# Up stage of a PEER layer: 32x32 block turns on VectorE in place of TensorE transposes, and an unsplit routing product

## The chip, the cores and the metric
One core of a Trainium2 chip runs one layer on 512 tokens. The metric is the device time of one execution in microseconds (us). The kernel before was timed three times: 4906.25, 4911.32 and 4913.47 us, median 4911.32 us.

## The reference, cut to what matters
The layer has a token-mixing half (attention, Fourier branch, output projection, layer norm) and a channel-mixing half. The second half, PEER, is what changes:

```python
def _peer(h, wq, keys, u, v):
    q = (hf @ wq).reshape(T, PEER_HEADS, 2, PEER_HALF)
    s = jnp.einsum('thpd,hpkd->thpk', q, keys)
    s1, i1 = lax.top_k(s[:, :, 0], 16);  s2, i2 = lax.top_k(s[:, :, 1], 16)
    cand_s = (s1[..., :, None] + s2[..., None, :]).reshape(T, 8, 256)
    cand_i = (i1[..., :, None] * 128 + i2[..., None, :]).reshape(T, 8, 256)
    top_s, pos = lax.top_k(cand_s, 16)
    idx = jnp.take_along_axis(cand_i, pos, axis=-1)
    w = jax.nn.softmax(top_s, axis=-1)
    a = jnp.einsum('td,thkd->thk', hb, u[ib])          # u: 16384 experts x 2048
    coef = wb * jax.nn.gelu(a, approximate=False)
    return jnp.einsum('thk,thkd->td', coef, v[ib])     # v: 16384 x 2048
```

All of it is fp32.

## The kernel before, in words
The order of work on each engine is written out by hand, engine by engine, with semaphores between them; there is no scheduler.

For 384 of the 512 tokens (TD) PEER is computed densely: every expert's activation is formed (the up stage), multiplied with a routing matrix that is zero but for the chosen experts, and multiplied with v (the down stage). The first 128 tokens (TS) instead gather the rows they chose.

**Up stage.** 128 blocks (NK) of 128 experts. For each block:
- SyncE loads 1 MB of u into `pu[s]`, one of two buffers (`pre_load`, L530 to L533), and stores the block's activations to DRAM (`pre_store`, L535 to L537). In its order stands load i+2, then store i, then load i+3. A load waits until the block that had the buffer is turned (`u_turned`); a store waits for gelu i (`gelu_set`).
- TensorE turns the 16 pieces of 128x128 into PSUM (`pre_turn`, L2175), a quarter of the next block ahead of each quarter of this one, and does the 48 products of the block with the activations in three split parts (`mm3`, L114 to L116: high times high, high times low, low times high). A quarter is 4 turns and 12 products.
- ScalarE copies the turned block to SBUF (`pre_copy`, L1049), rounds it to the high part (`pre_hi`, L1056) and takes the gelu of the product (`pre_gelu`, L1061). In one block (`top_block`, L1070) these stand: copy and high part of half 0 of block i+1, copy of half 1, gelu of block i, high part of half 1.
- GpSimd forms the low part (`u_low`, L698).

Beside the blocks run three other pieces of work, one after the other:
- Blocks 0 to 25 (P0 = 26): VectorE picks the experts (`top_experts`), once for each 128 tokens, four times.
- Blocks 26 to 49: routing. For each group of 4 tokens VectorE makes one-hot matrices (`one_hots`: four instructions of 128x512, L1651 to L1657), TensorE does 8 products (L2235, L2236), ScalarE copies them out (L1096) and SyncE stores 1 MB for each block (L544). Four groups go with each block.
- Blocks 50 to 127 (LATE = 50): GpSimd gathers 128 times 1 MB of u rows (`gather_u`, L707) into a ring of 4 buffers, and VectorE takes the dot products (L1673).

Earlier parts that the change touches: SyncE's loads of the output projection (L498 to L504), the layer norm output `xn2` (L1518), and the loads of the PEER query weights (`w2raw`, L518). Each of these has its channels in natural order, channel 128c + p in chunk c at partition p.

Of the kernel before, what the change touches and what calls it, by code (L numbers as in the profile page):

```python
# [55 lines left out]
TK_FIRST, TK_REST = 8, 6  # L56
P0 = TK_FIRST + TK_REST * DB
# [61 lines left out]
def layer_kernel(nc, a, out):  # L119
# [10 lines left out]
    with ctx:  # L130
# [3 lines left out]

        gelu_d = nc.dram_tensor("gelu_scratch", [P, NK, TD], fp32, kind="Internal").ap()
# [108 lines left out]
        smalls = sb("tk_smalls", 87.5, [P, 3, PH])
        wait_pad = sb("wait_pad", 87.875, [P, 1])
# [8 lines left out]
        chwh, chwl = sb("chwh", 200, [P, TD], f32r), sb("chwl", 201.5, [P, TD], f32r)  # L254
        oneJe = [sb(f"oneJe{s}", 84 + 2 * s, [P, 4, P]) for s in range(2)]
        oneI = [sb(f"oneI{s}", 40 + 2 * s, [P, 4, P], f32r) for s in range(2)]
        oneJh = [sb(f"oneJh{s}", 44 + 2 * s, [P, 4, P], f32r) for s in range(2)]
        oneJl = [sb(f"oneJl{s}", 48 + 2 * s, [P, 4, P], f32r) for s in range(2)]
        RT = 64
        route = [sb(f"route{s}", (168, 52)[s], [P, NK, RT]) for s in range(2)]  # L260

        pu = [sb(f"pu{s}", 136 + 8 * s, [P, D]) for s in range(2)]
        pT = sb("pT", 96, [P, DC, P])
        pTuh, pTul = sb("pTuh", 152, [P, DC, P], f32r), sb("pTul", 160, [P, DC, P], f32r)
# [8 lines left out]
        col = [sb(f"col{s}", 82 + 3 * s, [P, 2, TD], f32r) for s in range(2)]  # L273
# [7 lines left out]
        diag2 = sb("diag2", 200, [P, 4, P])  # L281
# [56 lines left out]
        tk_chain, iota_in, tk_diff, tk_exp, tk_chosen, ch_turned, ch_set, chw_hi, chw_set = (  # L338
            sem(n) for n in ("tk_chain", "iota_in", "tk_diff", "tk_exp", "tk_chosen", "ch_turned", "ch_set", "chw_hi", "chw_set"))
# [34 lines left out]
        def _(sp):
# [134 lines left out]
            wq_v = a["peer_wq"][0].rearrange("(c p) n -> p c n", p=P)  # L509
# [16 lines left out]
            flat = lambda t, k: t[bass.ds(k, 1)].rearrange("a j d -> (a j) d")  # L526
# [44 lines left out]
            for k in range(2):  # L571
                pre_load(LATE + 2 + k, k)
                route_store(GROUPS, 1, 2 * k)
                route_store(GROUPS, 1, 2 * k + 1)
                pre_store(LATE + k, k)
# [75 lines left out]
        def _(pool):  # L651
# [69 lines left out]
            k = 0  # L721
            for i in range(LATE + 2, NK):
                for h in range(2):
                    u_low(i, h)
                    if k < SLOTS and (2 * i + h) % 6 != 5:
                        gather_u(k)
                        k += 1
            while k < SLOTS:
                gather_u(k)
                k += 1  # L730
# [7 lines left out]
        def _(act):  # L738
# [291 lines left out]
            q_split(NO, 1, 16 * 49)  # L1030
            q_split(NO + 1, 0, 16 * 51)
# [763 lines left out]
        def _(pe):  # L1795
# [373 lines left out]
            def pre_turn(i, s, q):  # L2169
# [6 lines left out]
                if q % 2 == 1:  # L2176
                    mm.then_inc(u_turned, 1)
# [166 lines left out]
```

## Time and profile before

| | |
|---|---|
| median of the timed runs | 4911.32 us |
| span of the profiled execution, first to last instruction | 4908.6 us |
| TensorE busy | 4529.0 us, 92% |
| VectorE busy | 2830.0 us, 58% |
| ScalarE busy | 1645.8 us, 34% |
| GpSimd busy | 1578.3 us, 32% |
| first gelu of the up stage, last gelu | 2263.1 us, 3697.0 us |

The profile gives the profiled execution no time of its own beside this span; the span lies inside the scatter of the three timed runs. Busy time is the union of an engine's instructions. Matmuls overlap in the pipeline, so a row's duration says less than the distance from one start to the next. SPq is SyncE's queue: a row there is the issue of a transfer, not its landing.

### The profile page before, as it was taken

How to read it: one execution, taken by the hardware profiler on the slowest of the kernel's cores; microseconds unless marked ns; L12 is line 12 of the kernel's file. 1: busy time of each engine (PE TensorE's matmuls, PEld its weight loads, DVE VectorE, ACT ScalarE, POOL GpSimd, SP SyncE). 2: the span in 40 equal slices, each digit the busy share in tenths (PEclk: the TensorE clock that was granted, in tenths of full speed). 3: DMA queues.
4: the chain of work that ended last, by engine and by line, in shares of the span. 5: the costliest groups of instructions: out<-in, count | busy, mean ns of one | idle time of the engine just before them, and what ended most of it. 6: DMA issues, size and time to landing. Idle time of an engine off the chain costs nothing.

```text
span 4908.6 us, 61497 instructions
## 1 busy us (share of the span) xinstructions
PE 4529.0 (92%) x23115; PEld 3858.2 (79%) x23115; DVE 2830.0 (58%) x3097; ACT 1645.8 (34%) x1746; POOL 1578.3 (32%) x643
## 2 busy tenths in 40 slices
PE   7899998999989999599999998999997999999997
PEld 2587777777767877488999998999995777777776
DVE  1234665545436653657789944444444677787777
ACT  0322232333331121224446543444442233332232
POOL 0002332000002310223544557887782233323320
PEclk9899999999989999699999999999998999999998
DMA  8325664000015652453336677777776999989885
GB/s 283 100 77 174 181 184 142 16 30 30 32 39 156 187 173 66 137 167 108 117 110 151 167 225 282 292 292 286 291 282 228 358 335 336 333 330 337 340 331 177
DMA packets 652126, 967.09 MB, mean 197 GB/s; under 512 B 122203, under 2 KB 520595, under 8 KB 599571
## 3 DMA queue, kind: packets, MB, share of 16 engines
q1 hardware_dynamic: 610979, 680.35, 42.0%
q0 software_dynamic: 40928, 285.23, 15.6%
q8 instruction: 45, 0.74, 0.1%
q10 hardware_dynamic: 144, 0.52, 0.0%
q14 instruction: 30, 0.25, 0.0%
HBM read 896.82 MB, written 69.21 MB: 197 GB/s over the span
## 4 chain that ended last, share of the span: by engine, by line
PE 55%; DMA 14%; DVE 11%; issue 10%; POOL 5%; ACT 4%; SPq 1%; DVEq 0%; ACTq 0%; POOLq 0%
PE pp L114 16%; PE pp L116 15%; PE pp L115 15%; DMA gel<-gelu_scratch 11%; POOL pTul L698 4%; DVE acc L1686 3%; PE pp L2175 3%; DVE vDl L1407 3%; DMA wm<-in_w_mod_dram 1%; PE pp L1806 1%; DVE mred L1287 1%; PE pp L1964 1%; PE pp L2236 1%; PE pp L2235 1%; ACT wh L776 1%
## 5 line engine op out<-in xcount | busy, mean ns | idle before, releaser
L698 POOL TENSOR_TENSOR pTul<-pT,pTuh 128x1024 fp32r<-128x1024 f32 x256 | 743.0, 2902 | 508.6 <-ACT pTuh L1056 494.7
L114 PE MATMUL pp<-h2h,pTuh 128*128 128x384 f32 x2048 | 733.0, 358 | 18.5 <-POOL pTul L698 17.5
L114 PE MATMUL pp<-vDh,coh 128*128 128x512 f32 x1536 | 617.7, 402 | 94.3 <-DVE col L1407 93.7
L116 PE MATMUL pp<-h2h,pTul 128*128 128x384 f32 x2048 | 691.7, 338 | 0.0
L115 PE MATMUL pp<-h2l,pTuh 128*128 128x384 f32 x2048 | 690.1, 337 | 0.0
L1673 DVE SCALAR_TENSOR_TENSOR ring<-ring,h2tok 128x2048 f32<-128x2048 f32 x128 | 347.8, 2720 | 490.0 <-DMA ring<-in_peer_u_dram,sidx 489.5
L115 PE MATMUL pp<-vDl,coh 128*128 128x512 f32 x1536 | 610.9, 398 | 0.0
L116 PE MATMUL pp<-vDh,col 128*128 128x512 f32 x1536 | 610.1, 397 | 0.0
L674 POOL TENSOR_TENSOR mbuf<-mbuf,silu 128x2048 f32<-128x2048 f32 x64 | 261.1, 4080 | 1003.4 <-DMA mbuf<-in_w_mod_dram 1002.7
L712 POOL DMA_INDIRECT ring<-in_peer_v_dram,sidx x128 | 319.1, 2493 | 771.0 <-DVE acc L1686 752.9
L1126 ACT ACTIVATE vDh<-vraw 128x2048 fp32r<-128x2048 f32 x128 | 245.3, 1917 | 668.4 <-PE pp L116 409.8
L114 PEld LDWEIGHTS pp<-vDh,coh 128*128 128x128 f32 x1536 | 296.9, 193 | 179.5 <-DVE vDl L1407 63.6
L114 PEld LDWEIGHTS pp<-h2h,pTuh 128*128 128x128 f32 x2048 | 387.9, 189 | 27.9 <-POOL pTul L698 27.5
L1202 DVE TENSOR_TENSOR wl<-wraw,wh 128x2048 fp32r<-128x2048 f32 (+1 forms) x97 | 263.1, 2712 | 246.2 <-ACT wh L776 245.9
L1049 ACT ACTIVATE pT<-pp 128x1024 f32<-128x1024 f32 x256 | 265.3, 1036 | 396.8 <-PE pp L2175 395.3
L115 PEld LDWEIGHTS pp<-h2l,pTuh 128*128 128x128 f32 x2048 | 388.6, 190 | 0.0
L116 PEld LDWEIGHTS pp<-h2h,pTul 128*128 128x128 f32 x2048 | 386.6, 189 | 0.0
L116 PEld LDWEIGHTS pp<-vDh,col 128*128 128x128 f32 x1536 | 296.0, 193 | 63.6
L115 PEld LDWEIGHTS pp<-vDl,coh 128*128 128x128 f32 x1536 | 296.5, 193 | 61.0
L1407 DVE TENSOR_TENSOR vDl<-vraw,vDh 128x2048 fp32r<-128x2048 f32 x128 | 292.7, 2287 | 73.0 <-ACT vDh L1126 73.0
L2175 PE MATMUL pp<-ident,pu 128*128 128x128 f32 x2048 | 312.3, 276 | 17.9 <-DMA pu<-in_peer_u_dram 17.1
L114 PE MATMUL pp<-hxh,wh 128*128 128x512 f32 x784 | 315.1, 402 | 13.6 <-DVE wl L1202 9.8
(343 smaller groups left out, 8849.3 us busy)
## 6 DMA issues: line engine op xcount, KB each, us to landing
pu<-in_peer_u_dram SPq DMA_DIRECT2D x128, 1024.0 KB, 6.8
vraw<-in_peer_v_dram SPq DMA_DIRECT2D x128, 1024.0 KB
mbuf<-in_w_mod_dram SPq DMA_DIRECT2D x64, 1024.0 KB, 5.7
wraw<-in_w_in_dram SPq DMA_DIRECT2D x48, 1024.0 KB, 8.3
wt<-route_scratch SPq DMA_DIRECT2D x128, 384.0 KB
gel<-gelu_scratch SPq DMA_DIRECT2D x128, 384.0 KB
wm<-in_w_mod_dram SPq DMA_DIRECT2D x16, 2048.0 KB, 8.4
gelu_scratch<-act_g SPq DMA_DIRECT2D x128, 192.0 KB
```

What stands on the lines that cost most here:

```text
L114: pe.matmul(out, lh, rh, start=first, stop=False)
L115: pe.matmul(out, lh, rl, start=False, stop=False)
L116: return pe.matmul(out, ll, rh, start=False, stop=last)
L674: pool.tensor_tensor(mbuf[s][:, :, :], mbuf[s][:, :, :], silu[:, :, 0:1].to_broadcast([P, DC, P]), ALU.mult).then_inc(mu_prod, 1)
L698: pool.tensor_tensor(pTul[:, c, :], pT[:, c, :], pTuh[:, c, :].bitcast(fp32), ALU.subtract).then_inc(u_lo, 1)
L712: pool.indirect_dma_start(ring[k % 4][:, :], None, v_rows, bass.IndirectOffsetOnAxis(ap=sidx[:, k:k + 1], axis=0)).then_inc(ring_in[k % 4] ...
L1049: act.activation(pT[:, 8 * h:8 * h + 8, :], pp[h][:, :].rearrange("p (c j) -> p c j", c=8), ACT.Copy).then_inc(pre_raw, 1)
L1126: act.activation(vDh[s][:, :, :], vraw[s][:, :, :], ACT.Copy).then_inc(w_hi, 1)
L1202: dve.tensor_tensor(wl[s][:, 0:n, :], wraw[s][:, 0:n, :], wh[s][:, 0:n, :].bitcast(fp32), ALU.subtract).then_inc(w_lo, 1)
L1407: return dve.tensor_tensor(dst, src, hi.bitcast(fp32), ALU.subtract)
L1673: dve.scalar_tensor_tensor(out=chunks(ring[k % 4]), in0=chunks(ring[k % 4]), scalar=1.0, in1=h2tok[:, :, 0:TS], op0=ALU.mult, op1=ALU.mult ...
L2175: mm = pe.transpose(pb[q][:, P * (c % 4):P * (c % 4) + P], pu[s][:, P * c:P * c + P], ident[:, :])
```

## The change
- A load of a block is four transfers of 32 partitions each. Partition 32k + s takes channels 512k to 512k + 511 of experts s, 32 + s, 64 + s and 96 + s: pieces of 2 KB, where before each partition took one expert's whole row of 8 KB.
- VectorE turns the block in 32x32 squares, SBUF to SBUF, in two instructions of 128x1024 for each block (`u_turn`). TensorE's `pre_turn` and ScalarE's `pre_copy` are gone. `pT`, `pTul` and `pTuh` now have two buffers each; `pTul` lies in the same memory as `pT`.
- In this layout partition 32k + r of chunk c is channel 512k + 32c + r. So that the other operand has the same order, `xn2` is written in permuted order, the query weights are loaded by quarters of 32 partitions, and shift and scale go through DRAM once to be read back in the new order (`mod2`).
- The four `top_experts` run beside 40 blocks (TK = 10 each), with 20 turns placed between their steps; routing runs beside blocks 40 to 63, and the gathers beside blocks 66 to 127, two for each block and three for each of the first four.
- The routing weight is no longer split: four VectorE instructions of 128x128 make the weighted one-hot, one of 128x512 the other, and TensorE does 4 fp32 products in place of 8 of a split pair.

```diff
-TK_FIRST, TK_REST = 8, 6
-P0 = TK_FIRST + TK_REST * DB
+TK = 10
+P0 = TK * (DB + 1)
...
+            sp.wait_ge(mu_set, 3)
+            for w, at in enumerate((M_SH2, M_SC2)):
+                sp.dma_start(mod_d[w].rearrange("(c p) -> p c", p=P), modT[:, at:at + DC, 0],
+                             allow_slow_non_contiguous=True).then_inc(mod_kept, 16)
             sp.dma_start(ln_g[:, :], a["ln1_g"][0:1, :].to_broadcast([P, D])).then_inc(ln_in, 16)
             sp.dma_start(ln_b[:, :], a["ln1_b"][0:1, :].to_broadcast([P, D])).then_inc(ln_in, 16)
+            sp.wait_ge(mod_kept, 32)
+            for k in range(4):
+                for w in range(2):
+                    sp.dma_start(mod2[32 * k:32 * k + 32, w, :],
+                                 mod_d[w, QD * k:QD * k + QD].rearrange("(c r) -> r c", r=32),
+                                 allow_slow_non_contiguous=True).then_inc(mod_in, 16)
...
-                    sp.dma_start(w2raw[s][:, :, :], wq_v[:, :, bass.ds(i * (2 * P) + (1 - s) * P, P)]).then_inc(w_in_[s], 16)
+                    for k in range(4):
+                        sp.dma_start(w2raw[s][32 * k:32 * k + 32, :, :],
+                                     wq_v[k][:, :, bass.ds(i * (2 * P) + (1 - s) * P, P)]).then_inc(w_in_[s], 16)
...
             def pre_load(i, s):
                 if not isinstance(i, int) or i >= 2:
                     sp.wait_ge(u_turned, 2 * i - 2)
-                sp.dma_start(pu[s][:, :], flat(u_v, i)).then_inc(u_in[s], 16)
+                for k in range(4):
+                    sp.dma_start(pu[s][32 * k:32 * k + 32, :, :],
+                                 u_quarter[k][bass.ds(i, 1)].rearrange("a s b d -> (a s) b d")).then_inc(u_in[s], 16)
...
-            def pre_copy(i, h):
...
+            def pre_hi(i, s, h):
                 act.wait_ge(u_turned, 2 * i + h + 1)
+                if not isinstance(i, int) or i >= 2:
+                    act.wait_ge((u_half, a_done)[h], i - 1)
+                act.activation(pTuh[s][:, 8 * h:8 * h + 8, :], pT[s][:, 8 * h:8 * h + 8, :], ACT.Copy).then_inc(u_hi, 1)
...
-            def top_block(i, s, exp=None):
-                pre_copy(i + 1, 0)
-                pre_hi(i + 1, 0)
+            def up_block(i, s, exp=None):
+                pre_hi(i + 1, 1 - s, 1)
                 if exp is not None:
                     act.wait_ge(tk_diff, exp)
                     act.activation(best[:, :, :], best[:, :, :], ACT.Exp).then_inc(tk_exp, 1)
-                pre_copy(i + 1, 1)
+                pre_hi(i + 2, s, 0)
                 pre_gelu(i, s)
-                pre_hi(i + 1, 1)
...
+            def u_turn(i, s, h):
+                c = slice(8 * h, 8 * h + 8)
+                dve.wait_ge(u_in[s], 32 * (i - s) + 64)
+                if not isinstance(i, int) or i >= 2:
+                    dve.wait_ge((u_half, a_done)[h], i - 1)
+                dve.transpose(pT[s][:, c, :].rearrange("p c (b j) -> p b c j", b=4),
+                              pu[s][:, :, 256 * h:256 * h + 256].rearrange("p b (c j) -> p b c j", j=32)).then_inc(u_turned, 1)
...
+            def route_block(i, s, g):
+                one_hots(g, 0)
+                one_hots(g + 1, 1)
+                u_turn(i + 1, 1 - s, 1)
+                one_hots(g + 2, 0)
+                one_hots(g + 3, 1)
+                u_turn(i + 2, s, 0)
...
+            for i in range(LATE, NK):
+                if i + 1 < NK:
+                    u_turn(i + 1, (i + 1) % 2, 1)
+                for k in range(rows_before(i), min(rows_before(i) + 1, rows_before(i + 1))):
+                    dot(k)
+                if i + 2 < NK:
+                    u_turn(i + 2, i % 2, 0)
+                for k in range(rows_before(i) + 1, rows_before(i + 1)):
+                    dot(k)
...
-                    pe.matmul(o, oneJh[s][:, t, :], oneI[s][:, t, :], start=True, stop=False)
-                    mm = pe.matmul(o, oneJl[s][:, t, :], oneI[s][:, t, :], start=False, stop=True)
+                    mm = pe.matmul(o, oneJ[s][:, t, :], oneI[s][:, t, :], start=True, stop=True)
```

ScalarE in the first blocks of the up stage, before. `pT<-pp` is the copy out of PSUM, `pTuh<-pT` the high part, `act_g<-pp` the gelu of the block before the one whose parts stand around it.

```order
L1049 ACTIVATE pT<-pp 128x1024 [waits u_lo,u_turned]
L1056 ACTIVATE pTuh<-pT 128x1024 [waits u_half,pre_raw]
L1049 ACTIVATE pT<-pp 128x1024 [waits u_lo,u_turned]
L1061 ACTIVATE act_g_218<-pp 128x384 [waits g_stored1,a_done]
L1056 ACTIVATE pTuh<-pT 128x1024 [waits a_done,pre_raw]
```

The same place now:

```order
L1070 ACTIVATE pTuh_213<-pT_209 128x1024 [waits a_done,u_turned]
L1070 ACTIVATE pTuh_214<-pT_210 128x1024 [waits u_half,u_turned]
L1075 ACTIVATE act_g_216<-pp 128x384 [waits g_stored1,a_done]
L1070 ACTIVATE pTuh_214<-pT_210 128x1024 [waits a_done,u_turned]
L1070 ACTIVATE pTuh_213<-pT_209 128x1024 [waits u_half,u_turned]
L1075 ACTIVATE act_g_215<-pp 128x384 [waits g_stored0,a_done]
```

Before, the gelu of block i stood behind work on block i+1 alone. Now the row ahead of it is the high part of the first half of block i+2.

SyncE in the loop of the first stretch of the up stage, before. `pu` is the loaded block, `gelu_scratch` the store of a block's activations.

```order
L533 ISA [waits u_turned]
L533 DMA pu_212<-in_peer_u_dram 128x2048
L536 REGISTER_ALU
L537 ISA [waits gelu_set]
L537 DMA gelu_scratch<-act_g_217 128x384
L532 ISA
L533 ISA [waits u_turned]
L533 DMA pu_213<-in_peer_u_dram 128x2048
```

The same place now:

```order
L554 DMA pu_207<-in_peer_u_dram 32x4x512
L558 REGISTER_ALU
L559 ISA [waits gelu_set]
L559 DMA gelu_scratch<-act_g_215 128x384
L552 ISA
L554 ISA [waits u_turned]
L554 DMA pu_208<-in_peer_u_dram 32x4x512
L554 ISA
L554 DMA pu_208<-in_peer_u_dram 32x4x512
L554 ISA
L554 DMA pu_208<-in_peer_u_dram 32x4x512
```

The order of loads and stores is as before; each load is now four issues, with a register instruction ahead of each.

## Rows read from the trace of the kernel before

**Rows 1.** The page: the chain that ended last, by engine
```profile
PE 55%; DMA 14%; DVE 11%; issue 10%; POOL 5%; ACT 4%; SPq 1%; DVEq 0%; ACTq 0%; POOLq 0%
```

**Rows 2.** Busy us of PE, PEld, DVE, ACT, POOL; clock, DMA share, GB/s
```profile
2264.00:2520.00 256.00, 253.41 (x1605) 249.07 (x1604) 206.79 (x744) 124.57 (x139) 128.12 (x49) 1.00 0.34 122
2560.00:2860.00 300.00, 292.42 (x2059) 289.82 (x2058) 295.60 (x342) 180.54 (x193) 150.35 (x44) 1.00 0.64 158
2960.00:3680.00 720.00, 712.21 (x4428) 695.38 (x4429) 313.83 (x230) 314.50 (x345) 569.48 (x252) 1.00 0.76 285
```

**Rows 3.** Instructions that touch the gelu tile, duration min/median/max, first and last start
```profile
L1061 ACT ACTIVATE act_g<-pp x128: 491/492/494, 2263.1 to 3697.0; 128x384 f32<-128x384 f32 x128
```

**Rows 4.** TensorE in time order, start and us: one quarter, then a routing group
```profile
2352.24 0.60 PE L2175 MATMUL pp<-ident,pu 128*128 128x128 f32 x4
...
2352.85 0.34 PE L115 MATMUL pp<-h2l,pTuh 128*128 128x384 f32 x1
...
2354.77 0.60 PE L2175 MATMUL pp<-ident,pu 128*128 128x128 f32 x4
...
2601.96 0.22 PE L2235 MATMUL pp<-oneI,oneJh 128*128 128x128 f32 x1
...
2602.80 0.62 PE L2175 MATMUL pp<-ident,pu 128*128 128x128 f32 x4
```

**Rows 5.** SyncE's queue in time order, two blocks of the first stretch
```profile
2389.35 0.35 SPq L537 DMA_DIRECT2D gelu_scratch<-act_g  x1
2390.03 0.34 SPq L533 DMA_DIRECT2D pu<-in_peer_u_dram  x1
2399.41 0.35 SPq L537 DMA_DIRECT2D gelu_scratch<-act_g  x1
2400.53 0.34 SPq L533 DMA_DIRECT2D pu<-in_peer_u_dram  x1
```

**Rows 6.** From issue to landing of `pu` loads: 2240:2520, then 2950:3300
```profile
DMA to landing us min/median/max: 4.6/4.8/6.9
DMA to landing us min/median/max: 4.9/7.4/14.1
```

**Rows 7.** Transfers by line, whole span: count, KB each, median us to landing
```profile
w2raw<-in_peer_wq_dram SPq DMA_DIRECT2D x16, 1024.0 KB, 8.6
praw_kv<-in_w_ukv_dram SPq DMA_DIRECT2D x8, 1024.0 KB, 6.5
```

**Rows 8.** ScalarE, then SyncE, in time order, late in the up stage
```profile
3418.12 0.49 ACT L1061 ACTIVATE act_g<-pp 128x384 f32<-128x384 f32 x1 [1.15 <-PE pp L116]
3418.51 1.05 ACT L1056 ACTIVATE pTuh<-pT 128x1024 fp32r<-128x1024 f32 x1
3418.77 0.35 SPq L537 DMA_DIRECT2D gelu_scratch<-act_g  x1
```

**Rows 9.** VectorE in time order: first and last steps of one `top_experts`
```profile
2240.89 1.23 DVE L1600 COPY tk_sc<-score 128x2048 f32<-128x2048 f32 x1 [0.99 <-DMA iota<-in_k_iota_dram]
2297.13 2.29 DVE L1624 TENSOR_REDUCE tk_chosen<-tk_pick 128x128 f32<-128x2048 f32 x1
```

**Rows 10.** VectorE in time order, routing: one-hot steps, and one small TENSOR_SCALAR
```profile
2602.48 0.68 DVE L1657 TENSOR_TENSOR oneJl<-oneJe,chwl 128x512 fp32r<-128x512 f32 x1
2603.13 2.85 DVE L1651 TENSOR_TENSOR oneJe<-iota,chT 128x512 f32<-128x512 f32 x1
...
2279.19 0.22 DVE L1610 TENSOR_SCALAR tk_bpos<-tk_besti 128x128 uint32<-128x128 uint32 x1
```

**Rows 11.** Tiles `pTul` and `ring`, 2960:3690, ns min/median/max
```profile
L698 POOL TENSOR_TENSOR pTul<-pT,pTuh x139: 2375/2398/4514, 2969.9 to 3684.7; 128x1024 fp32r<-128x1024 f32 x139
L1673 DVE SCALAR_TENSOR_TENSOR ring<-ring,h2tok x117: 2280/2293/5167, 2958.9 to 3687.9; 128x2048 f32<-128x2048 f32 x117
```

**Rows 12.** The chain of waits in time order: output projection, and the late stretch
```profile
1784.26 10.34 DMA wraw<-in_w_out_dram
...
2943.52 17.56 DMA pu<-in_peer_u_dram
```

More of the change, by code:

```diff
@@ L252, in layer_kernel @@
         dots, scoef = sb("dots", 206, [P, SLOTS]), sb("scoef", 206.5, [P, SLOTS])
[L254 to L258, printed above, removed]
-        RT = 64
[L260 to L264, printed above, removed]
+        oneJ = [sb(f"oneJ{s}", 40 + 2 * s, [P, 4, P]) for s in range(2)]
+        oneI = [sb(f"oneI{s}", 44 + 2 * s, [P, 4, P]) for s in range(2)]
+        RT = 64
+        route = [sb(f"route{s}", (168, 48)[s], [P, NK, RT]) for s in range(2)]
+        pu = [sb(f"pu{s}", 136 + 8 * s, [P, 4, QD]) for s in range(2)]
+        pT = [sb(f"pT{s}", 152 + 8 * s, [P, DC, P]) for s in range(2)]
+        pTul = [sb(f"pTul{s}", 152 + 8 * s, [P, DC, P], f32r) for s in range(2)]
+        pTuh = [sb(f"pTuh{s}", (96, 80)[s], [P, DC, P], f32r) for s in range(2)]
         act_g = [sb(f"act_g{s}", (5.5, 204)[s], [P, TD]) for s in range(2)]
@@ L525, in _ @@
             v_v = a["peer_v"][0].rearrange("(i j) d -> i j d", j=NK)
-            flat = lambda t, k: t[bass.ds(k, 1)].rearrange("a j d -> (a j) d")
+            u_quarter = [u_v[:, :, QD * k:QD * k + QD].rearrange("i (b s) d -> i s b d", s=32) for k in range(4)]
             for ss in g_stored:
@@ L570, in _ @@
                 route_steps(r)
[L571 to L575, printed above, removed]
+            pre_load(LATE + 2, 0)
+            for k in range(4):
+                route_store(GROUPS, 1, k)
+            pre_store(LATE, 0)
+            pre_load(LATE + 3, 1)
+            pre_store(LATE + 1, 1)
             with sp.Fori(LATE // 2 + 1, LATE // 2 + 3) as i:
@@ L694, in _, with u_low @@
                     unit(s, 16 * m + 16)
-            def u_low(i, h):
+            def u_low(i, s, h):
                 c = slice(8 * h, 8 * h + 8)
                 pool.wait_ge(u_hi, 2 * i + h + 1)
-                pool.tensor_tensor(pTul[:, c, :], pT[:, c, :], pTuh[:, c, :].bitcast(fp32),
+                pool.tensor_tensor(pTul[s][:, c, :], pT[s][:, c, :], pTuh[s][:, c, :].bitcast(fp32),
                                    ALU.subtract).then_inc(u_lo, 1)
@@ L713, in gather_v @@
                     ap=sidx[:, k:k + 1], axis=0)).then_inc(ring_in[k % 4], 16)
-            with pool.Fori(0, LATE + 2) as i:
-                u_low(i, 0)
-                u_low(i, 1)
+            with pool.Fori(0, LATE // 2 + 1) as i:
+                for s in range(2):
+                    for h in range(2):
+                        u_low(2 * i + s, s, h)
             pool.wait_ge(tk_chosen, 2)
@@ L720, in _ @@
                 pool.wait_ge(ss, 64 * (TD // RT // 2) + 16)
-            k = 0
             for i in range(LATE + 2, NK):
[L723 to L730, printed above, removed]
+                for k in range(rows_before(i), rows_before(i) + 1):
+                    gather_u(k)
+                u_low(i, i % 2, 0)
+                for k in range(rows_before(i) + 1, rows_before(i + 1)):
+                    gather_u(k)
+                u_low(i, i % 2, 1)
             for k in range(SLOTS):
@@ L1617, in top_experts @@
                 for w in range(2):
+                    turn(14 + 3 * w)
                     tk.link(dve.tensor_tensor(
@@ L1620, in top_experts @@
                         iota[:, 0:TOPK].unsqueeze(1).to_broadcast([P, PH * TOPK, TOPK]), ALU.is_equal))
+                    turn(15 + 3 * w)
                     pv = pick[:, :, :].rearrange("p (h k) m -> p h k m", h=PH)
@@ L2165, in _, with pre_quarter @@
             mod_sum(63, 1, 6, 30)
-            def pre_turn(i, s, q):
-                if q == 0:
-                    pe.wait_ge(u_in[s], 8 * (i - s) + 16)
-                if q % 2 == 0 and (not isinstance(i, int) or i >= 1):
-                    pe.wait_ge(pre_raw, 2 * i - 1 + q // 2)
-                for c in range(4 * q, 4 * q + 4):
-                    mm = pe.transpose(pb[q][:, P * (c % 4):P * (c % 4) + P], pu[s][:, P * c:P * c + P], ident[:, :])
-                if q % 2 == 1:
-                    mm.then_inc(u_turned, 1)
-            def pre_up(i, s, q):
+            def pre_quarter(i, s, q):
                 if q == 0 and (not isinstance(i, int) or i >= 2):
@@ L2214, in _ @@
             pe.wait_ge(mu_set, 4)
-            for i in range(TK_FIRST):
+            for i in range(TK):
                 pre_block(i, i % 2)
```

232 lines of the change are left out of this document (121 added, 111 removed).

## The prediction, made before the changed kernel was run
> **What bounds the kernel now.** First the chain that ended last, by engine: TensorE has 55% of it [rows 1]. Then the busy time by stretch. The up stage has three: experts being picked, routing, and gathers. TensorE is busy for 253.4 of 256 us in the first and 712.2 of 720 in the last; in the routing stretch VectorE is the full one, 295.6 of 300 [rows 2]. Third, the place of the stage: from its first gelu at 2263.1 to its last at 3697.0 are 1433.9 us for 127 steps [rows 3]. The two TensorE-bound stretches take about 10.1 us a block: one quarter runs from 2352.24 to 2354.77, 2.53 us, four to a block [rows 4]. Last, the DMA queue, which is never full (share 0.34, 0.64, 0.76 [rows 2]), but whose order of issue I read closely: store i, then load i+3, ten us apart [rows 5].
>
> **What TensorE and VectorE gain and pay.** Between 2352.85 and 2354.77 stand 11 products, 0.174 us each; 12 of them make 2.09 us, so without the four turns and the change of operand a quarter loses 0.44 us and a block falls from 10.1 to 8.4 us. Over 128 blocks that is 220 us of TensorE time. In routing a group now takes 0.84 us (2601.96 to 2602.80 [rows 4]) for 8 products of 128 columns. No row shows a plain fp32 product of 128 columns with 128 rows; I take four of them as dear as the eight (bounds 0.4 and 1.7 us), so a block there needs 4 x (2.09 + 0.09 + 0.84 + 0.07) = 12.4 us.
> VectorE gets two turns a block. The trace has none. A 128x2048 copy takes 1.23 us, a 128x2048 reduce 2.29 us [rows 9]; for half that size 0.6 and 1.15 us, and a full 2.3 us if a turn took two passes. I take 1.2 us, nearest to the one-pass row. One picking of experts lasts from 2240.89 to 2299.42, 58.5 us [rows 9]; with 20 turns 83 us in 10 blocks, 8.3 a block. In routing, 16 small steps of 0.22, four wide ones of 0.68 and two turns are 8.6 us; the wide ones and GpSimd hold each other up (0.68 becomes 2.85 [rows 10]), and two `pTul` steps of 2.40 [rows 11] make it at most 13.4. Late: two dot products of 2.29 and two turns, 7.0 us, and again up to 4.8 behind GpSimd. ScalarE loses its copies and is idle half the time. So by busy times alone the stage would shrink.
>
> **What the new order makes of the loads.** Here I expect the end to be set. ScalarE now takes gelu i behind the high part of block i+2, half 0. That waits for its turn, the turn for load i+2; store i waits for gelu i; and load i+3 stands behind store i in SyncE's order. So load i+2 must land before load i+3 is issued: one load under way at a time, one round of this circle for each block. Before, gelu i waited only for block i+1, whose load had gone out a whole block earlier: two blocks for each round, and TensorE was the slower. The terms of one round:
> - gelu to issue of the store: 3418.12 to 3418.77, 0.65 us [rows 8]; store to load 0.68 and 1.12 us, mean 0.90 [rows 5]. Together 1.55 us.
> - Issue to landing. A load of whole rows lands in 4.8 us in the first stretch [rows 6]. The new one is four issues of 32 partitions in pieces of 2 KB. The nearest row is `praw_kv`, 1 MB in 2 KB pieces, 6.5 us; 512-byte pieces take 8.6 us [rows 7]. I take 6.5 and 0.3 for the later issues, 6.8 us; ends 4.8 and 8.6.
> - the turn 1.2; the high part 1.05 less the 0.1 by which ScalarE overlaps its steps [rows 8], 0.95; two hand-overs of 0.1.
> Sum 1.55 + 6.8 + 1.2 + 0.95 + 0.2 = 10.7 us, above TensorE's 8.4 and VectorE's 8.3. TensorE follows in the shadow, some 2 us idle a block.
> The Trainium skill (SBUF — State Buffer, Door 1: The DMA port swizzle) says that 32 partitions reach 8 of the 16 DMA ports: 189 GB/s against 328 at 1 MiB, and that several transfers do not add up. By it a load costs 2.3 us more than the whole-row one, 7.1 us, and the forecast would be some 30 us later; no row here shows a transfer of 32 partitions.
>
> **The sum, from first gelu to last.** 40 blocks of 10.7: 428 us. 24 of routing: circle 10.7 + one copy-out of about 1.1, TensorE 12.4, VectorE up to 13.4: I take 12.7, 305 us. 63 late: landing there was 7.4 in place of 4.8 us in the first part and somewhat less later [rows 6], so 2.3 on top: 13.0 us each, 819 us. Once, where the loads of v stand ahead, a load takes 17.56 us [rows 12], 12 more than usual, and is now on the circle: 12 us. The exponentials' table loads, four times 1.5: 6 us. Total 1570 against 1434: +136 us.
> Outside: SyncE now waits between the norm's loads and the next `wraw` load, a load that is on the chain (10.34 us from 1784.26 [rows 12]). Two stores of 2048 single numbers, their landing and eight issues put it off by about 10 us, and as the norm's rows are through by then it lands some 4 sooner: +6 us (ends 0 and 15). The first `w2raw`, in four parts, +2 us (the others have a whole block of slack). `xn2` may lose a faster mode, within 1 us each, inside the 6. The down stage is left as it is.
> Profiled span 4908.6 + 136 + 8 = 5053 us. The median stands 2.7 us above the span, inside the scatter, so I say 5050 us. That is slower by 2.8%.
>
> **Rivals.**
> 1. The circle is there, but loads land as quickly as now, 4.8 + 0.3 = 5.1 us, because engines and not the destination set their pace. For it: the first and last stretch move whole rows at a DMA share of 0.34. Rounds of 9.0 and 11.3 us, routing 12.4: 360 + 298 + 712 + 18 = 1388, -46; 4871 us. Between it and the forecast each us of landing is worth 103 us, and equality lies at 5.5 us. Against: both rows with smaller pieces are dearer.
> 2. No circle: the load runs ahead after all and the other engines decide. First stretch VectorE 8.3 with small waits, 8.7, 348 us; routing 12.4, 298; late, dots and `pTul` in turn 9.4, with hand-overs 9.8, 617 us, and 18: 1281, -153. With +8 outside 4766 us. For it stands only that the waits might be met early; against, the order of three queues, in which I find no way round.
> 3. Turns are dearer, 2.3 us. The circle gains 1.1 on 103 blocks: +113, 5165 us. For it: nothing in the trace says that a turn runs at the rate of a reduce. The Trainium skill (VectorE: DVE Perf Modes, The three transpose paths) gives 311 ns for 128x128 in 32x32 squares of bf16; eight of these would be 2.5 us, which by itself would put the time near 5185 us, and no row here shows one.
> TensorE's clock was granted in full in all three stretches [rows 2]. Idle for 2 to 5 us a block it may be cut at times; it has that much slack, so I put no price on it.
>
> **Chances and range.** Forecast 52% (own range 4950 to 5130), rival 1 20%, rival 2 14%, rival 3 14%. A difference of 0.2%, 10 us, is what can be told from none. Faster: rival 2 and most of rival 1, 0.28. Within: 0.04. Slower: 0.68. The range 4860 to 5180 leaves out rival 2 and the far end of rival 3, 2 in 10.
>
> **What would show it.** Right: load issues 10 to 11 us apart in the first stretch and 13 late; each turn of a first half released by the DMA; landing of the last quarter about 7 us after the first issue; TensorE busy for about 80% in the first stretch and 65% in the last; the chain running through `pu`, the turn, `pTuh`, the gelu and SyncE. Wrong: a load issued while the one before is under way; TensorE full at 8.4 us a block (rival 2); landing near 5 us (rival 1); a turn of 2 us or more (rival 3).

## The result and the profile after

The changed kernel takes 5054.99 us (median of 4 runs, 5044.2 to 5068.84); the kernel before takes 4910.3 us beside it. The ratio is 1.0288, 95% interval 1.0274 to 1.0303. Forecast were 5050 us and a ratio of 1.028. The profiled execution has a span of 5067.2 us, 12 us over the median, where the one of before lay within 3 us of its own median. So the traces differ by 158.6 us and the medians by 145, and what is read from the traces below is up to 14 us too much in sum.

The page of the changed kernel: busy time, share and instructions; then the chain that ended last, by engine.

```profile
PE 4391.1 (87%) x21067; PEld 3686.3 (73%) x21067; DVE 3052.9 (60%) x3412; ACT 1381.0 (27%) x1489; POOL 1591.9 (31%) x643
...
DMA 22%; DVE 13%; issue 7%; SPq 5%; PE 4%; ACT 1%; POOL 0%; DVEq 0%; ACTq 0%; POOLq 0%
```

The shares of this chain sum to 52%: it reaches back to 2362 us only, and can't be set against the 55% of TensorE in [rows 1], which are of a whole span. The chain within the up stage can, first before (2263 to 3697), then now (2293 to 3861):

```profile
by line: PE pp L114 15.9%; PE pp L116 15.5%; PE pp L115 15.5%; issue 14.9%; POOL pTul L698 12.6%; PE pp L2175 9.1%; PE pp L2236 2.8%; PE pp L2235 2.6%; POOL ring L707 2.5%; DVE oneJl L1657 1.9%; DMA pu<-in_peer_u_dram 1.9%; ACT pTuh L1056 1
...
by line: DMA pu<-in_peer_u_dram 35.0%; issue 16.4%; DVE oneJ L1700 8.7%; DVE pT L1607 8.7%; SPq L554 8.5%; ACT act_g L1075 2.7%; SPq L559 2.7%; DVE oneI L1701 1.3%; PE pp L115 1.2%; PE pp L116 1.1%; PE pp L117 1.1%; DVEq L1700 1.0%; SPq L56
```

TensorE's lines fall from 61% of the stage to about 3%, and the loads of `pu`, VectorE's steps and SyncE's queue take their place. The gelu tile and the three stretches of the changed kernel, columns as in [rows 2, 3]:

```profile
L1075 ACT ACTIVATE act_g<-pp x128: 467/473/539, 2293.8 to 3860.6; 128x384 f32<-128x384 f32 x128
```
```profile
2300.00:2740.00 440.00, 350.78 (x1874) 339.04 (x1873) 305.55 (x866) 109.07 (x130) 202.53 (x76) 0.93 0.46 108
2780.00:3060.00 280.00, 276.89 (x1739) 255.27 (x1738) 278.88 (x475) 136.05 (x152) 114.98 (x44) 1.00 0.76 171
3200.00:3840.00 640.00, 495.94 (x2551) 467.86 (x2552) 415.92 (x320) 132.66 (x160) 499.92 (x214) 0.95 0.94 278
```

The up stage takes 1566.8 us for 1433.9. In the first stretch no engine is full: TensorE is busy for 80% (350.78 of 440), and its granted clock, which was 1.00 before, averages 0.93: for short stretches it is at the lower of its two levels, 1.2 GHz. In the last it is busy for 77%. In the routing stretch VectorE is full, 278.88 of 280, and TensorE nearly so, 276.89.

One round of the first stretch, first SyncE's queue, then ScalarE and VectorE (start and us; in brackets idle time and its end), answering to [rows 5, 8]:

```profile
2397.20 0.37 SPq L559 DMA_DIRECT2D gelu_scratch<-act_g  x1
2398.12 2.27 SPq L554 DMA_DIRECT2D pu<-in_peer_u_dram  x4
2408.45 0.37 SPq L559 DMA_DIRECT2D gelu_scratch<-act_g  x1
2409.12 1.82 SPq L554 DMA_DIRECT2D pu<-in_peer_u_dram  x4
2419.58 0.37 SPq L559 DMA_DIRECT2D gelu_scratch<-act_g  x1
```
```profile
2406.85 1.06 ACT L1070 ACTIVATE pTuh<-pT 128x1024 fp32r<-128x1024 f32 x1 [4.82 <-DVE pT L1607]
2407.82 0.47 ACT L1075 ACTIVATE act_g<-pp 128x384 f32<-128x384 f32 x1
...
2405.57 1.25 DVE L1607 STREAM_TRANSPOSE pT<-pu 128x1024 f32<-128x1024 f32 x1 [0.38 <-DMA pu<-in_peer_u_dram]
...
2416.70 1.25 DVE L1607 STREAM_TRANSPOSE pT<-pu 128x1024 f32<-128x1024 f32 x1 [4.61 <-DMA pu<-in_peer_u_dram]
```

Load at 2398.12, landed at 2405.57 (7.45 us), turn, high part at 2406.85, gelu at 2407.82, store at 2408.45, next load at 2409.12: 11.0 us, every link right behind the last. The chain of waits says the same in one view, in time order:

```profile
2410.62 6.06 DMA pu<-in_peer_u_dram
2416.70 1.26 DVE pT L1607
...
2418.95 0.48 ACT act_g L1075
2419.58 0.37 SPq L559
...
2420.50 0.32 SPq L554
...
2422.00 5.99 DMA pu<-in_peer_u_dram
```

The reader sees a circle with one load in it. The last of the four issues stands 1.5 us behind the first and lands 6.0 us later.

### The profile page after: what moved, and what is told of

Same layout as the page of the kernel before. It is cut to its first block, busy times and chain, and to the rows that moved or that the text cites. A ratio compares the mean times of both kernels' runs of the same rounds, so it can differ in the third digit from the quotient of the medians.

```text
span 5067.2 us, 58390 instructions
## 1 busy us (share of the span) xinstructions
PE 4391.1 (87%) x21067; PEld 3686.3 (73%) x21067; DVE 3052.9 (60%) x3412; ACT 1381.0 (27%) x1489; POOL 1591.9 (31%) x643
## 4 chain that ended last, share of the span: by engine, by line
DMA 22%; DVE 13%; issue 7%; SPq 5%; PE 4%; ACT 1%; POOL 0%; DVEq 0%; ACTq 0%; POOLq 0%
DMA gel<-gelu_scratch 11%; DMA pu<-in_peer_u_dram 11%; DVE acc L1749 3%; DVE oneJ L1700 3%; DVE pT L1607 3%; SPq L554 3%; DVE vDl L1418 3%; PE pp L115 1%; PE pp L116 1%; PE pp L117 1%; ACT act_g L1075 1%; SPq L559 1%; SPq L608 0%; SPq L615 0%; DVE oneI L1701 0%
## 5 line engine op out<-in xcount | busy, mean ns | idle before, releaser
L721 POOL TENSOR_TENSOR pTul<-pT,pTuh 128x1024 fp32r<-128x1024 f32 x256 | 695.5, 2718 | 603.0 <-ACT pTuh L1070 601.6
L116 PE MATMUL pp<-h2l,pTuh 128*128 128x384 f32 x2048 | 711.0, 347 | 0.0
L117 PE MATMUL pp<-h2h,pTul 128*128 128x384 f32 x2048 | 711.0, 347 | 0.0
L115 PEld LDWEIGHTS pp<-h2h,pTuh 128*128 128x128 f32 x2048 | 404.8, 198 | 312.8 <-POOL pTul L721 286.3
L1607 DVE STREAM_TRANSPOSE pT<-pu 128x1024 f32<-128x1024 f32 x256 | 317.2, 1240 | 449.2 <-DMA pu<-in_peer_u_dram 385.7
L1070 ACT ACTIVATE pTuh<-pT 128x1024 fp32r<-128x1024 f32 x256 | 271.5, 1060 | 1146.7 <-DVE pT L1607 1146.4
L735 POOL DMA_INDIRECT ring<-in_peer_v_dram,sidx x128 | 337.2, 2634 | 752.5 <-DVE acc L1749 732.9
L116 PEld LDWEIGHTS pp<-h2l,pTuh 128*128 128x128 f32 x2048 | 405.7, 198 | 0.0
L117 PEld LDWEIGHTS pp<-h2h,pTul 128*128 128x128 f32 x2048 | 403.8, 197 | 0.0
L1725 DVE SCALAR_TENSOR_TENSOR ring<-ring,h2tok 128x2048 f32<-128x2048 f32 x128 | 359.2, 2810 | 0.0
L115 PE MATMUL pp<-hxh,wh 128*128 128x512 f32 x784 | 316.3, 404 | 13.7 <-DVE wl L1213 9.8
```

What stands on the lines that cost most here:

```text
L115: pe.matmul(out, lh, rh, start=first, stop=False)
L116: pe.matmul(out, lh, rl, start=False, stop=False)
L117: return pe.matmul(out, ll, rh, start=False, stop=last)
L721: pool.tensor_tensor(pTul[s][:, c, :], pT[s][:, c, :], pTuh[s][:, c, :].bitcast(fp32), ALU.subtract).then_inc(u_lo, 1)
L735: pool.indirect_dma_start(ring[k % 4][:, :], None, v_rows, bass.IndirectOffsetOnAxis(ap=sidx[:, k:k + 1], axis=0)).then_inc(ring_in[k % 4] ...
L1070: act.activation(pTuh[s][:, 8 * h:8 * h + 8, :], pT[s][:, 8 * h:8 * h + 8, :], ACT.Copy).then_inc(u_hi, 1)
```

## The experiments

The table sets them side by side. The ratio is to the kernel before, run on the same chip. The three columns on the right are the mean distance from one gelu's start to the next, in us, from the trace: blocks 0 to 40, 40 to 64, 64 to 127 (in e10, which has the block numbers of the kernel before, routing is blocks 26 to 49). In brackets is the median of blocks 20 to 30, the steady pace. In e6, e7 and e8 the pieces of u lie in another arrangement than the turns are made for, so their up products are not the layer's; the kind and amount of work are the same.

| kernel | us | ratio (95%) | first | routing | late |
|---|---|---|---|---|---|
| changed | 5055.0 | 1.0288 (1.0274-1.0303) | 11.7 (11.4) | 12.9 | 12.5 |
| e1 gelu first | 4899.4 | 0.9977 (0.9966-0.9988) | 9.5 (8.3) | 12.7 | 11.5 |
| e2 load ahead | 4866.4 | 0.9904 (0.9887-0.9922) | 8.9 (8.5) | 12.7 | 11.4 |
| e3 loads of rows late | 5048.8 | 1.0283 (1.0265-1.0302) | 11.8 (11.3) | 12.9 | 12.4 |
| e5 rows behind `w_out` | 5032.1 | 1.0237 (1.0216-1.0258) | 11.7 (11.3) | 12.9 | 12.5 |
| e4 128 partitions, 4 outermost | 6037.5 | 1.2294 (1.2273-1.2315) | 16.9 (16.6) | 18.0 | 22.6 |
| e6 one issue, 8 KB rows | 4890.7 | 0.9955 (0.9937-0.9973) | 9.6 (8.7) | 12.8 | 11.2 |
| e7 32 partitions, 8 KB rows | 4995.1 | 1.0161 (1.0139-1.0183) | 11.1 (10.6) | 12.9 | 12.0 |
| e8 128 partitions, 2 KB | 4928.5 | 1.0033 (1.0022-1.0044) | 10.2 (9.6) | 12.8 | 11.5 |
| e9 two queues | 4970.0 | 1.0133 (1.0110-1.0157) | 10.2 (9.6) | 12.8 | 12.1 |
| e10 before, unsplit routing | 4903.4 | 0.9989 (0.9978-1.0001) | - | 13.8 | - |
| e11 e1 + e2 + e5 | 4833.5 | 0.9852 (0.9836-0.9868) | 8.7 (8.3) | 12.7 | 11.2 |
| e12 e11, low parts first | 4836.0 | 0.9845 (0.9831-0.9859) | 8.7 (8.3) | 12.7 | 11.3 |

The code below is shortened.

**Is there a circle? e1 and e2.** Each opens it at another place, and changes no transfer and no arithmetic.

```
e1, up_block, and the same in route_part:
-                pre_hi(i + 2, s, 0)
                 pre_gelu(i, s)
+                pre_hi(i + 2, s, 0)
```


> The changed kernel with one swap on ScalarE: gelu i ahead of the high part of block i+2, half 0. Theory (circle through pu, turn, high part, gelu, store, next load): the circle is opened, two loads can be under way. First stretch from 11.7 to about 8.8 us a block (TensorE 8.4, VectorE 8.3), routing unchanged at 12.9 (VectorE bounds it), late stretch from 12.5 to about 10.5: 4830 us (4780 to 4880). Rival A (loads of 32 partitions share one path, two under way land half as fast each): first stretch about 9, late unchanged at 12: about 4940. Rival B (VectorE's fixed order bounds the blocks, not the loads): no change, 5055 within 15.


```
e2, SyncE, and likewise in its other loops:
+            pre_load(2, 0)
             with sp.Fori(0, P0 // 2) as i:
                 for s in range(2):
-                    pre_load(2 * i + 2 + s, s)
+                    pre_load(2 * i + 3 + s, 1 - s)
                     pre_store(2 * i + s, s)
```


> The changed kernel with SyncE's order shifted by one: load i+3 is issued before store i, not behind it; ScalarE's order stays. It opens the same circle at another place. Theory: the gain of the ScalarE swap within 60 us, so 4780 to 4890. If the ScalarE order alone were the trouble (gelu held back by late high parts, and not the load behind the store), this would stay above 4980. Rival B (VectorE's order): no change, 5055 within 15.

Measured: 4899 and 4866 us, 156 and 189 less than the changed kernel. That is the circle, and both rivals fall: the first stretch goes from 11.4 to 8.3 and 8.5 us a block, which is TensorE's own pace. In e2 the chain of waits of 2320 to 2600 runs through TensorE's products, where in the changed kernel (2320 to 2740) it ran through the loads (its chain starts at 2362, so some 10% of that window stands in no term):

```profile
by line: PE pp L115 23.8%; PE pp L116 23.6%; PE pp L117 23.6%; issue 5.9%; DVE tk_pick L1679 4.6%; DVE tk_pick L1673 4.2%; DVE tk_chosen L1681 3.2%; DVE tk_besti L1594 3.0%; DVE tk_best L1589 2.9%; DVE pT L1611 2.5%; DVE tk_chosen L1685 0.6
```
```profile
by line: DMA pu<-in_peer_u_dram 31.1%; issue 23.7%; SPq L554 9.0%; DVE pT L1607 8.5%; ACT act_g L1075 3.1%; SPq L559 2.8%; PE pp L115 1.7%; PE pp L116 1.6%; PE pp L117 1.6%; ACT L1075 1.2%; DVE tk_chosen L1677 1.1%; DVE tk_cand L1596 0.9%; 
```

e1 stays 20 us over the range I gave. Its steady pace is right, but blocks 20, 30 and 40, where a picking of experts ends, take 20 to 23 us in it and 13 to 17 in e2; why was not followed up.

The late stretch stops at 10.8 us in both, and there another pair of engines is full. GpSimd and VectorE of e2, in time order:

```profile
3398.60 2.39 POOL L725 TENSOR_TENSOR pTul<-pT,pTuh 128x1024 fp32r<-128x1024 f32 x1
3401.15 2.83 POOL L734 DMA_INDIRECT ring<-in_peer_u_dram,sidx  x1 [0.16 <-issue]
3404.00 2.39 POOL L725 TENSOR_TENSOR pTul<-pT,pTuh 128x1024 fp32r<-128x1024 f32 x1
...
3398.84 4.30 DVE L1729 SCALAR_TENSOR_TENSOR ring<-ring,h2tok 128x2048 f32<-128x2048 f32 x1
3403.08 1.23 DVE L1611 STREAM_TRANSPOSE pT<-pu 128x1024 f32<-128x1024 f32 x1
3404.24 4.30 DVE L1729 SCALAR_TENSOR_TENSOR ring<-ring,h2tok 128x2048 f32<-128x2048 f32 x1
```

A dot product of 2.29 us [rows 11] takes 4.30 beside GpSimd's step of 2.39, and the gather's issue 2.83 in place of the 0.96 that it takes where VectorE waits. Each half block is then 5.4 us on both engines. Windows of e11, 3200 to 3600: VectorE busy for 392.5 of 400 us, GpSimd for 383.2. A rival is the DMA engines, whose share is about 1 there. Here are the columns of [rows 2] for e2, and then for e6, which moves as much a second in whole rows:

```profile
3200.00:3600.00 400.00, 329.61 (x1769) 306.25 (x1767) 382.61 (x221) 90.98 (x109) 382.11 (x148) 1.00 1.03 306
...
3250.00:3600.00 350.00, 289.41 (x1559) 268.61 (x1557) 350.00 (x196) 81.36 (x98) 338.45 (x130) 1.00 0.81 308
```

In e6 the DMA share is 0.81, and the steady pace is 10.8 us all the same, with VectorE busy for all of the 350 us. So it is not the DMA engines.

**What does the landing cost? e4, e6, e7, e8, e9.** The circle stays, and the load's form changes.

```
e4:  for b in range(4):
+        dma(pu[s][:, b, :], u[i] as (k s) d)      # 4 x 32 rows: outermost 4
e6:  dma(pu[s] as p (b d), u[i])                   # one issue, 128 rows of 8 KB
e7:  for k in range(4):
+        dma(pu[s][32k:32k+32] as p (b d), u[i, 32k:32k+32])
e8:  for k in range(4):
+        dma(pu[s][:, k, :], u[i, :, 512k:512k+512])   # outermost 128
e9:  SyncE issues k = 0, 1 as before; ScalarE, behind gelu i, k = 2, 3
```


> The changed kernel with the same bytes of u in the same four issues of 2 KB pieces, but each issue fills all 128 partitions with one piece (cut by row group, not by channel quarter). Theory for the landing (what an issue of 32 partitions lacks is spread: its packets go to half of the destination's ways): landing of the last quarter falls from 7.5 to about 5.5 us, the circle by 2 us in the first and late stretch, 103 blocks: 4850 us (4820 to 4900). Rival 1 (the size of the pieces sets it): landing and time unchanged, 5055 within 20. Rival 2 (the number of issues sets it): the same as rival 1 here; rows in one issue would tell them apart.

> The changed kernel with each block of u loaded as before the change: one issue, 128 partitions, rows of 8 KB (the turns then work on another arrangement of u, so that the values of the up products differ; nothing of the work is left out). Theory (a faster landing is worth its time on the circle until TensorE or VectorE bounds): landing from 7.5 to about 5.2 us; first stretch 9.0 a block, late 10.8: 4870 us (4840 to 4910). Rival (the loads' landing does not set the pace): 5055 within 15.

> As the run before it, but in four issues of 32 partitions with rows of 8 KB (values as there). Theory (32 partitions of destination set the pace of the packets): no gain over the changed kernel, landing 7 to 7.5 us, 5050 within 20. Rival (pieces of 2 KB set it): the time of the run with one issue of whole rows, 4870, at most 40 more for three further issues.

> Four issues of 2 KB pieces, each over all 128 partitions, with 128 as the outermost count of both sides; where the earlier run of this kind had 4 outermost and only 4 completion packets for each issue, here 16 are expected (values differ as in the two runs before). Theory: landing 5.2 to 5.6 us, 4880 (4850 to 4920). Rival (size of the pieces): landing 7.5, 5055 within 20. If the earlier 11 us burst came from cutting by row group and not from the outermost 4, it returns here: 6040.

> The changed kernel, its circle left in place, but quarters 2 and 3 of each load are issued by ScalarE's DMA queue right behind gelu i (quarters 0 and 1 by SyncE behind the store, as they are), so that two issues of different partitions can be under way at once. Theory (each issue of 32 partitions is held by its own part of the destination, different parts add up): packets near 84 ns in place of 147, last landing about 5.5 us after SyncE's issue and ScalarE's half 1.5 us sooner: first stretch from 11.25 to 9.3 a block, late from 12.0 to 11: 4920 us (4890 to 4970). Rival (transfers of several queues do not add up, the sum of bytes takes the same 5.8 us): the earlier half alone gains about 1 us a block, 4960 to 5000. No gain at all, 5055, if the last issue's landing is set by SyncE's half.

e4 missed by a thousand us and taught most. It carries the bytes of the changed kernel to the same places, but each issue has an outermost count of 4, and the trace shows 4 small completion packets for it where the others have 16: four of the sixteen engines carry it. The queue's line of three kernels in 2300 to 2500 (packets, MB, share of 16 engines' time), the changed kernel, e4 and e8:

```profile
q1 hardware_dynamic: 12383, 21.42, 46.3%
```
```profile
q1 hardware_dynamic: 8020, 14.85, 19.8%
```
```profile
q1 hardware_dynamic: 14285, 24.70, 37.4%
```

Per MB the changed kernel spends 2.16% of the engines' time in these 200 us, e8 1.51% and e4 1.33%. So e4's packets are quick, but one engine has four times as many in a row: a load takes 11.4 us from its first packet to its last, where one of the changed kernel takes 5.8 and one of e8 4.4. The Trainium skill has the rule (DMA: Bandwidth & Descriptors, Why a DMA increments its semaphore by 16 and not by 1): the number of engines is the largest up to 16 that divides the slowest dimension of both sides. It agrees with the 4 and the 16 seen here. e8 has the same four issues of 2 KB pieces over all partitions with 128 outermost, and its steady pace is 1.8 us better than the changed kernel's. That is the price of 32 partitions; the kernel's time, 4928, is 8 us over the range I had given. The pieces of 2 KB cost 0.8 (changed kernel against e7). If the costs simply add, three more issues cost 0.1, what is left of the 0.9 between e8 and e6; no run tests that sum, since the 1.9 between e7 and e6 follows from the other three differences. e6's 8.7 also stands close to TensorE's 8.4, which may hide a part of its gain. The landing line of e6, 2350 to 2550, then of the changed kernel, one quarter each, 2300 to 2740:

```profile
DMA to landing us min/median/max: 4.6/4.8/5.8
```
```profile
DMA to landing us min/median/max: 3.8/5.1/6.3
```

The line of the changed kernel counts each quarter from its own issue; 1.5 us and the queue of the three before it come on top. Whole loads, from the first issue to the first turn, take 7.6 us in the changed kernel (median of 2300 to 2740), 6.8 in e7, 5.7 in e8 and 5.0 in e6 (2300 to 2600). e7's theory said "no gain" and e7 gained 60 us: pieces do count, as the prediction had it, but partitions count more. e6, at 4891, is the first rival of the prediction made real (4871): with the landing left alone the change would have gained 0.45%.

The Trainium skill (SBUF — State Buffer, Door 1: The DMA port swizzle) gives 189 GB/s for a 1 MiB transfer to 32 partitions and 328 to 128. The runs agree in direction and show less of it: 2.16% against 1.51% is a factor of 1.4, where the page's figures make 1.7.

e9 fell between: 4970 us, at the edge of the theory's window and in the rival's. The ScalarE half is issued 2.2 us ahead of SyncE's. In the round at 2434 its packets run from 2435.77 to 2438.93 and SyncE's from 2438.39 to 2441.61, so the two hardly overlap, and the run doesn't tell whether two queues add up. That stays open.

**The detour of the norm's rows: e3 and e5.**

```
e3:
-            sp.wait_ge(mod_kept, 32)
-            (the eight loads of mod2)
             with sp.Fori(1, DC // 2) as i:          # loads of w_out
             ...
+            sp.wait_ge(mod_kept, 32)
+            (the eight loads of mod2)
e5: as e3, and the wait for mu_set and the two stores into mod_d go there too
```


> The changed kernel, with the wait for the two stores of the norm's rows and their eight loads moved behind the loads of w_out. Theory: the detour holds up the third w_out load, which came 32 us later in the profile, 25 to 30 of them not there before; the time falls by 25 us (18 to 32), 5030. Rival (the third w_out load is late for other causes, as the xres load of 4 MB ahead of it): 0 to 6 us, as the prediction priced it.

> The changed kernel with both the two stores of the norm's rows (4096 packets of 4 bytes) and their eight loads behind the loads of w_out. With the loads alone moved the time fell by only 6 us, and the w_out loads were still late: the next issue took 23.3 us behind the stores. Theory now: it is the stores that fill the queues for 16 us; with them gone from ahead of w_out the time falls by 25 us (18 to 32), 5030. Rival: the rows are then late for the norm's affine step, which takes back what w_out gains: 5045 to 5060.

e3 gained 6 us, which its interval can't tell from nothing, where I had expected 25: my reason was wrong. Not SyncE's wait holds up `w_out`, but what is in the queues. SyncE of the changed kernel, of e3, of e5:

```profile
1788.31 1.36 SPq L508 DMA_DIRECT2D mod_scratch<-modT  x2
1789.72 1.16 SPq L510 DMA_DIRECT2D ln_g<-in_ln_g_dram  x1
1790.92 0.43 SPq L511 DMA_DIRECT2D ln_b<-in_ln_b_dram  x1
1808.09 7.76 SPq L515 DMA_DIRECT2D mod<-mod_scratch  x8
1816.19 0.41 SPq L520 DMA_DIRECT2D wraw<-in_w_out_dram  x1
```
```profile
1787.23 0.39 SPq L514 DMA_DIRECT2D wraw<-in_w_out_dram  x1
1787.89 23.31 SPq L516 DMA_DIRECT2D wraw<-in_w_out_dram  x1
```
```profile
1785.70 0.39 SPq L510 DMA_DIRECT2D wraw<-in_w_out_dram  x1
1786.88 6.38 SPq L512 DMA_DIRECT2D wraw<-in_w_out_dram  x1
```

The transfers by line on the changed kernel's page (KB each, us to landing) name the culprit:

```profile
mod_scratch<-modT SPq DMA_DIRECT2D x2, 8.0 KB, 16.4
```

The two stores are 2048 packets of four bytes each and take 16.4 us; two megabytes of `ln_g` and `ln_b` stand behind them, and of e3's two loads of `w_out` after these the second hangs for 23.31 us. With the stores moved too, in e5, it is 6.38 (6.23 before the change), the time falls by 23 us, and the rows are ready at 1945, long before the norm asks at 2003.

**The routing part alone, e10.**

```
the kernel before, with
-  oneJe, oneJh, oneJl by four wide steps; two f32r products per token
+  for t in range(4): dve.tensor_scalar(oneJe[:, t], iota, chT[:, 1, at], chT[:, 2, at], is_equal, mult)
+  pe.matmul(o, oneJe[:, t], oneI[:, t])      # plain fp32
```


> The kernel before with one part of the change alone: the routing products unsplit (four fp32 products a group for eight, four small VectorE steps and one wide one for four wide ones). Theory (four fp32 products cost TensorE as much as the eight, VectorE has slack to gain): TensorE bounds the 24 blocks at 4 x (2.53 + 0.84) = 13.5 us, from 13.9 before: -10 us, 4900 (4890 to 4912). Rival A: the fp32 products are dearer, 1.1 us a group: +1 us a block, 4935. Rival B: they cost half, 0.42: 11.8 a block, 4860.

4903.4 us, as the theory said: TensorE is busy for 300.00 us of 300 there, and four fp32 products cost it what the eight did. In the changed kernel it is VectorE that bounds this stretch. The chain of waits of 2780 to 3060 runs mostly through its steps:

```profile
by line: DVE oneJ L1700 47.8%; issue 20.8%; DVE pT L1607 10.1%; DVE oneI L1701 6.9%; DVEq L1700 5.2%; DMA route_scratch<-route 3.0%; DMA pu<-in_peer_u_dram 2.4%; SPq L554 1.0%; DVEq L1701 1.0%; ACT route L1107 0.8%; SPq L559 0.3%; ACT act_g
```

TensorE is not far behind: from one group of routing products to the next it takes 2.97 us at the least and 3.22 at the median, four to a block, which makes 11.9 and 12.9 us a block. VectorE, then GpSimd:

```profile
2859.14 3.17 DVE L1700 TENSOR_SCALAR oneJ<-iota,chT 128x128 f32<-128x128 f32 x4
2862.23 0.68 DVE L1701 TENSOR_TENSOR oneI<-iota,chT 128x512 f32<-128x512 f32 x1
2862.83 1.23 DVE L1607 STREAM_TRANSPOSE pT<-pu 128x1024 f32<-128x1024 f32 x1
2863.99 1.07 DVE L1700 TENSOR_SCALAR oneJ<-iota,chT 128x128 f32<-128x128 f32 x4
...
2858.87 2.59 POOL L721 TENSOR_TENSOR pTul<-pT,pTuh 128x1024 fp32r<-128x1024 f32 x1 [3.86 <-ACT pTuh L1070]
```

Four small steps take 1.07 us, and 3.17 where GpSimd's step runs: 2 x (3.17 + 1.07 + 2 x 0.68 + 1.23) is 13.7, and less the overlaps of neighbours the 12.9 us of a block. No opening of the circle moved it: the steady blocks of e1, e2 and e11 take 12.9 too.

**A version that beats both: e11 and e12.**

> The changed kernel with the gelu swap, the load ahead of the store, and the norm's rows behind w_out, all three. Theory: the two swaps open the same circle, so the second adds little to the first (0 to 15 us); the rows are worth their own 23 us. From 4866: 4840 us (4825 to 4850), faster than the kernel before by 1.4%. Rival (each swap removes a wait of its own): the gains add, 4900 - 189 - 23 = 4690.


```
e12, GpSimd:
-            with pool.Fori(0, LATE // 2 + 1) as i:      # low parts, then the wait for r_stored
+            with pool.Fori(0, LATE // 2 + 2) as i:
```


> The run with both orders and the rows moved, with one more edit: GpSimd takes the low parts of two more blocks before it waits for the routing table's stores and starts the gathers. In the runs with the circle open it stood 19 us there with the low part of a block behind it. Theory (TensorE starves on that low part, so the stall is part of the 25 us block at the start of the late stretch): 15 us (8 to 20) less than 4833, 4818. Rival (VectorE waits in its order for the first gathered row anyway, and the stall moves there): within 6 of 4833.

e11 takes 4833.5 us, 1.5% less than the kernel before and 4.4% less than the changed one. The two swaps do not add: e2's 4866 less 23 for the rows is 4843, and 10 remain for the second swap, no more than the scatter of the runs (17 us in e11). e12 is the same within its interval, as its rival said. GpSimd's stall of 20.66 us is gone, but VectorE waits in its order for the first gathered row all the same, and the block of 23.7 us comes back one block later as 24.2. GpSimd of e11, then of e12:

```profile
2928.97 1.09 POOL L734 DMA_INDIRECT ring<-in_peer_u_dram,sidx  x1 [20.66 <-DMA route_scratch<-route]
```
```profile
2936.26 1.09 POOL L734 DMA_INDIRECT ring<-in_peer_u_dram,sidx  x1 [2.96 <-DMA route_scratch<-route]
```

## Why the prediction was right, and where only the sum was

- **The circle** was the cause of the first and the late stretch, with every link that was named; e1 and e2 show it. Rival 2 (no circle, 4766) is what e11 makes of the kernel: 8.7 us a block in the first stretch, as priced there, but 11.2 late where it had 9.8, since VectorE and GpSimd slow each other.
- **First stretch, 10.7 us x 40 = 428.** Measured 468.8. The term that was too small is the landing: 7.5 us for 6.8, and of what it has over whole rows most is the 32 partitions. That makes 11.3 a block, +25. The figures of the Trainium skill (SBUF — State Buffer, Door 1: The DMA port swizzle), by which the prediction put a load at 7.1 us, came nearer than the row of `praw_kv`, from which it took 6.5 and with the later issues 6.8. Another 16 us are single blocks longer than their neighbours, as the 17.6 us at block 40. Rival 1 rested in part on a misread row: the last stretch moves whole rows at a DMA share of 0.76 and not of 0.34 [rows 2].
- **The turn, 1.2 us**: 1.24 in 256 records; rival 3 is out.
- **Routing, 12.7 x 24 = 305.** Measured 308.7. The 12.7 was a value between TensorE's 12.4 and VectorE's 13.4, with no reason given for the point between; VectorE's steps decide. Their 13.4 counted two steps of GpSimd in full, and 2.1 us of each fall on VectorE.
- **Late, 13.0 x 63 = 819 and 12 for the loads of v.** Measured 789.3 with the latter. The steady pace is 11.9: of the 2.3 us that I added from the later landings of [rows 6] only 0.7 came; the last quarter lands 8.2 us behind the first issue at the median, for 7.5 in the first stretch. TensorE was busy for 77% and not for 65%. But the entry costs more than one wait: blocks 64 to 69 are 20.4, 17.6, 13.5, 19.1, 12.6 and 31.1 us, 43 over the steady pace. The last of them is the one with the loads of v ahead, priced at 12 and 19 us over the pace, with a wait of 22.02 us for its load. At the first of them SyncE stands for 14.12 us on four route stores and 3.56 on the next:

```profile
3063.59 14.12 SPq L566 DMA_DIRECT2D route_scratch<-route  x4
3077.75 3.56 SPq L559 DMA_DIRECT2D gelu_scratch<-act_g  x1
3081.36 1.88 SPq L554 DMA_DIRECT2D pu<-in_peer_u_dram  x4
```

- **The detour, 6 us (ends 0 and 15)**: 23 by e5, outside the ends. I priced the wait and the landing, and not the 4096 packets that stand ahead of `w_out`. `xn` kept its 1336 ns, and the first `w2raw` showed no loss.
- **The sum was luck in part.** +136 in the stage (measured +132.9) and +8 outside (+30.7, of which 5 lie ahead of the detour), the down stage 5 shorter. In the stage +41 and -42 cancel; outside the error of 17 is hidden by the profiled execution lying 12 over the median. Four blocks of table loads, 6 us, are in the measured paces already. And 4908.6 + 136 + 8 with the 2.7 us by which the median stood above the span is 5055, where the prediction wrote 5050. The sum was closer than its parts.

## What to carry to other kernels

Before an operation moves to an idle engine, draw the order of every in-order queue as one circle, from a load's issue through each engine back to the next issue, and count how many loads are in it; one swap of two lines was worth 3 to 4% here, and without it an estimated 220 us less of TensorE's work came out as 145 us more. A small or oddly cut transfer is priced by its packets, by how many engines carry them and by how many partitions they go to, not by its bytes. And where two engines slow each other, their busy times can't be summed apart: take each step's time from a row where the other runs.

## What the runs showed of the hardware that was not expected

- The number of engines that carried an issue followed the outermost count of its shape: 4 there, 4 completion packets, and 11.4 us from the first packet to the last for 1 MB in four issues (e4); 128 there, 16 packets and 4.4 us (e8).
- With 4096 packets of four bytes ahead of it on the queue, the fourth issue behind them took 23.31 us (e3), and 6.38 without them (e5).
- GpSimd's step of 2.6 us went with a small VectorE step of 2.42 us for 0.27, and with a dot product of 4.30 for 2.29; the gather's issue on GpSimd went from 0.96 to 2.83 us beside VectorE.
- TensorE's granted clock fell to 0.93 where it was busy for 80%, and was 1.00 in e11's first stretch, busy for 99% (277.56 of 280 us). The changed kernel's waits in the first stretch ended at the loads and not at TensorE, so little of its time can be put down to that clock.
